# Stick-breaking attention of a two-layer trunk: triangle sums issued ahead of the next pair's scores

## What is computed

```python
z = jnp.einsum("bthd,bshd->bhts", qb, kb) * scale            # scores
log_1m = jnp.where(causal, jax.nn.log_sigmoid(-z), 0.0)
log_survive = lax.cumsum(log_1m, axis=3, reverse=True) - log_1m
w = jnp.where(causal, jnp.exp(jax.nn.log_sigmoid(z) + log_survive), 0.0)
outs.append(jnp.einsum("bhts,bshd->bthd", w, vb))
```

## Time and profile before

| | |
|---|---|
| time, median of 3 runs | 803.9 us (803.72 to 804.56) |
| time of the profiled execution | 803.06 us |
| its span | 801.3 us |
| TensorE busy | 792.3 us (99%) |
| VectorE / ScalarE / GpSimd busy | 615.6 / 438.2 / 69.9 us |
| HBM | 176 GB/s over the span |
| granted TensorE clock | 1.00 (2.4 GHz) |

### The profile page before, as it was taken

One profiled execution on the slowest core, in us unless ns is written; L12 is line 12 of the kernel. 1 busy time (PEld: TensorE's weight loads), 2 busy tenths in 40 slices (PEclk: granted clock), 3 DMA queues, 4 the chain that ended last, 5 costly groups with the idle time before them and its releaser, 6 DMA issues.

```text
span 801.3 us, 9769 instructions
## 1 busy us (share of the span) xinstructions
PE 792.3 (99%) x3770; PEld 662.9 (83%) x3770; DVE 615.6 (77%) x925; ACT 438.2 (55%) x520; POOL 69.9 (9%) x94
## 2 busy tenths in 40 slices
PE   9999999999999999999999999999999999999998
PEld 7987788888888888888888888888888888888886
DVE  6688889998757688888747878588666778888862
ACT  5667775466536544544426576757653744445430
POOL 4001013540000000000000000113420000000000
PEclk9999999999999999999999999999999999999999
DMA  7854466443456566555555544443435565565551
GB/s 246 286 165 156 136 216 212 152 159 125 158 158 195 187 196 204 182 193 210 182 185 182 186 158 157 158 137 127 153 130 166 182 206 179 192 210 184 187 208 52
DMA packets 85293, 141.38 MB, mean 176 GB/s; under 512 B 3406, under 2 KB 50672, under 8 KB 85248
## 3 DMA queue, kind: packets, MB, share of 16 engines
q1 hardware_dynamic: 84256, 139.60, 53.2%
q10 hardware_dynamic: 608, 1.06, 0.4%
q0 software_dynamic: 384, 0.11, 0.1%
HBM read 139.68 MB, written 1.07 MB: 176 GB/s over the span
## 4 chain that ended last, share of the span: by engine, by line
PE 77%; DVE 12%; ACT 5%; issue 3%; DMA 2%; SPq 0%; DVEq 0%; ACTq 0%
PE acc L1317 24%; PE acc L1319 24%; PE acc L1318 24%; DVE lo L978 4%; PE bank L1314 2%; DVE zs L1089 2%; DMA raw<-in_ssd_w_in 2%; ACT hi L661 1%; ACT zs L661 1%; DVE seg L1109 1%; ACT sq L661 1%; DVE seg L1117 1%; PE bank L1505 1%; PE bank L1483 1%; DVE hg L1109 1%
## 5 line engine op out<-in xcount | busy, mean ns | idle before, releaser
L978 DVE TENSOR_TENSOR lo<-raw,hi 128x2048 fp32r<-128x2048 f32 (+2 forms) x132 | 295.2, 2242 | 77.7 <-ACT hi L661 76.7
L661 ACT ACTIVATE hi<-raw 128x2048 fp32r<-128x2048 f32 (+2 forms) x132 | 244.8, 1861 | 93.4 <-DMA raw<-in_ffn_w_gate_up 44.1
L1317 PE MATMUL acc<-lo,aT_hi 128*128 128x512 f32 (+1 forms) x672 | 262.2, 390 | 0.5 <-DVE lo L978 0.4
L1319 PE MATMUL acc<-hi,aT_lo 128*128 128x512 f32 (+1 forms) x672 | 258.6, 385 | 0.0
L1318 PE MATMUL acc<-hi,aT_hi 128*128 128x512 f32 (+1 forms) x672 | 258.3, 384 | 0.0
L1319 PEld LDWEIGHTS acc<-hi,aT_lo 128*128 128x128 f32 x672 | 126.1, 188 | 25.5
L1317 PEld LDWEIGHTS acc<-lo,aT_hi 128*128 128x128 f32 x672 | 126.2, 188 | 25.3 <-DVE lo L978 0.6
L1318 PEld LDWEIGHTS acc<-hi,aT_hi 128*128 128x128 f32 x672 | 126.3, 188 | 24.3
L1196 DVE STREAM_TRANSPOSE uT<-un 32x256 f32<-32x256 f32 (+1 forms) x192 | 79.4, 414 | 3.1
L1317 PE MATMUL acc<-lo,uT_hi 128*128 128x512 f32 x176 | 68.6, 390 | 0.0
L1319 PE MATMUL acc<-hi,uT_lo 128*128 128x512 f32 x176 | 68.5, 389 | 0.0
(11 more groups left out here) (205 smaller groups left out, 851.7 us busy)
## 6 DMA issues: line engine op xcount, KB each, us to landing
raw<-in_ffn_w_gate_up SPq DMA_DIRECT2D x88, 512.0 KB, 4.7
raw<-in_ffn_w_down SPq DMA_DIRECT2D x22, 1024.0 KB, 4.9
raw<-in_sb_w_in SPq DMA_DIRECT2D x20, 1024.0 KB, 5.1
raw<-in_ssd_w_in SPq DMA_DIRECT2D x14, 1024.0 KB, 5.2
raw<-in_mem_w_kv SPq DMA_DIRECT2D x8, 1024.0 KB, 5.0
raw<-in_ssd_w_out SPq DMA_DIRECT2D x8, 1024.0 KB, 4.9
raw<-in_sb_w_out SPq DMA_DIRECT2D x8, 1024.0 KB, 4.9
seg<-cs_rows SPq DMA_DIRECT2D x6, 384.0 KB, 5.1
```

Source lines behind the costliest of these rows:

```text
L661: return nc.scalar.activation(out_, in_, func, **k)
L978: v.tensor_tensor(lo[w % RING][:, c], raw[w % RING][:, c], hi[w % RING][:, c].bitcast(F), ALU.subtract).then_inc(lo_ready, 1)
L1317: mm(ps, stat_hi, mov_lo, start=first, stop=False)
L1319: return mm(ps, stat_lo, mov_hi, start=False, stop=last)
```

## The change

In the units that hold both the scores of a new pair and the triangle sums of the pair before (83, 85, 87, 89, 91) the steps `sps`, `C`, `C` stand ahead of `z`, `z` in the plan. Nothing else in the code changes; the bank numbers follow from the plan.

```diff
@@ -179,12 +179,13 @@
     u = block_end("v0") + 1
     pairs = SB_HEADS // 2
     for i in range(pairs + 1):
+        if i > 0:
+            b = 2 * i - 1
+            at(u + 2 * i, ("sps", b), ("C", b - 1), ("C", b))
         if i < pairs:
             at(u + 2 * i, ("z", 2 * i), ("z", 2 * i + 1))
             at(u + 2 * i + 1, ("zd", 2 * i), ("zd", 2 * i + 1))
         if i > 0:
-            b = 2 * i - 1
-            at(u + 2 * i, ("sps", b), ("C", b - 1), ("C", b))
             at(u + 2 * i + 1, ("O", b - 1), ("O", b))
```

## The result

The changed kernel takes 805.66 us (median of 7 runs, 805.42 to 806.84) against 803.72 us (median of 7, 803.03 to 804.56): ratio 1.0027, 95% interval 1.0017 to 1.0037, that is 0.27% or 2.2 us slower, the distance between the means; the medians are 1.94 us apart. The profiled executions stand at 805.51 us (span 803.7) and 803.06 us (span 801.3), 2.4 us apart. The forecast was 806.6 us, with 0.85 for slower.

What follows compares the result with a forecast made beforehand. TensorE, busy 99% of the span, was taken to bound the kernel. Delays of 1.59 and 1.12 us sum to 2.7, on 803.9 giving 806.6 us (+0.34%); own range 805.9 to 807.3, 8 in 10 from 804.7 to 808.3.

Steps and rivals of the forecast that it cites:

- The bound: Whole span: TensorE is busy 99%; its delays between 508 and 607 us are added to the end in full.
- C is ready earlier: Units 83 to 94: C, issued 1.2 us earlier, still finds sp_lo written; slack 1.66 us in unit 83, 1.1 for C2.
- ScalarE: Unit 83: z's calls fall behind C's exps, so |z| of heads 2 and 3 starts at 528.23, 4.5 us later.
- Banks: Units 84 and 88: the hT transposes now wait for z's banks; in unit 84 these free at 531.81 and 532.86 us.
- The sum: Delays of TensorE in units 84 and 88: 1.59 + 1.12 = 2.7 us, bounds 2.0 to 3.4.
- first term: Unit 84: second hT q1 transposes start at 532.96 instead of 531.37 us, delaying everything behind by 1.59 us.
- second term: Unit 88: second hT q2 transposes start at 565.65 instead of 564.53 us, another 1.12 us.
- The waits named as signs: Transposes wait for VectorE's spb: 0.9 and 0.7 us in unit 84, about 0.4 and 0.7 in unit 88.
- Only the first place stalls: Rival: ScalarE and VectorE catch up by unit 87, so unit 88 loses nothing; +1.0 to +1.6 us, 805.4; chance 0.12.
- No slower: Rival: VectorE's subtraction of C starts earlier in units 83 and 87, O0's wait goes; 803.3 us, -0.6; chance 0.06.
- C waits for softplus: Rival: sp_lo comes late, C2 and C6 wait 0.3 to 0.9 us each; +4 to +6 us, 808.5; chance 0.13.
- the clock falls: Rival: a TensorE wait lowers its granted clock and slows the products behind it; +3 us or more; chance 0.02.

Runs made afterwards that it cites:

- TensorE's order alone: Against the kernel before: only TensorE issues C ahead of z, bank deal and ScalarE's sequence as before; 803.46 us against 803.11, ratio 1.0004.
- TensorE's order back: Against the changed kernel: TensorE issues z ahead of C again, banks and ScalarE as changed; 805.75 us, ratio 1.0028 to the kernel before.
- unit 83 alone: The kernel before with the new order of steps only in unit 83; 804.57 us against 803.11, ratio 1.0019.
- banks as before: Against the changed kernel: banks dealt out in the old order, TensorE and ScalarE as changed; 809.2 us, ratio 1.0066 to the kernel before.
- ScalarE's order back: Against the changed kernel: ScalarE does z's six calls ahead of C's exps again, TensorE and banks as changed; 803.09 us, ratio 0.9995 to the kernel before.

## Why the prediction was right

- **The bound.** Every wait of TensorE is paid in full at the end: the last stretch lies between 232.30 and 232.42 us in all ten kernels, which is no difference for spans given to 0.1 us. Shown.
- **C is ready earlier, TensorE's order is free.** No wait for `sp_lo` in any run; TensorE's order alone leaves the distances as they were. C2 was due 1.26 us behind the end of `sp_lo` (538.72 against 536.50 + 0.96), where 1.1 was worked out.
- **ScalarE.** |z| at 528.08, worked out 528.23; with the 0.16 us by which this execution is early it agrees to 0.01. Shown by its own edit.
- **Banks.** The transposes wait for L1219 at both places, and with the old deal the O products do. Shown.
- **O0** keeps its wait, 0.56 us.
- **The sum.** 1.59 + 1.12 = 2.71 us were worked out, 1.53 + 1.03 = 2.56 measured. In the first term, the part that was mis-sized is the handover from the release of a bank to TensorE's start: I took the 0.10 us seen from GpSimd to TensorE, and from VectorE it is 531.69 - 531.64 = 0.05. In the second term the handover cancels, since it also sets when TensorE arrives; there 0.06 of the 0.09 us is the subtraction, 559.14 + 0.16 = 559.30 instead of 559.36. The remaining 0.01 and 0.03 us are too small to be traced.
- **The waits named as signs.** Two pairs of L1315 for `spb` came, at both places, but smaller than named: 0.68 and 0.40 us instead of 0.9 and 0.7, then 0.18 and 0.40 instead of 0.4 and 0.7. The named sizes were delays of a start, and the profile counts as a wait only the time in which TensorE stands idle. The sum was made with the delays, so it holds.
- **From the profile to the median.** 806.6 us was forecast and 805.66 came. Of the 0.94 us, 0.15 is the sum and 0.18 the base (803.9 was the median of three runs, 803.72 that of seven). The other 0.6 us is the difference between the medians' distance, 1.94, and the traces', 2.56. By the medians the loss is just outside the forecast's own band of +2.0 to +3.4 us, and 805.66 just below its 805.9; by the distances it is well inside. Seven executions spread over 1.4 us, so that chance can do this is likely, but argued. Where more were run, the two measures agree better: 2.53 by medians and 2.62 by distances with TensorE's order back (9 and 25 executions), 1.46 and 1.53 with unit 83 alone (11 and 33). The run with banks as before doesn't fit that, 5.98 against 4.80.
- **Rivals.** "Only the first place stalls" is ruled out by the 1.03 us in unit 88, and the run with unit 83 alone shows what it would have given, 1.0019. "No slower" rested on an earlier subtraction; the changed plan gives none, but the edit that brings it, 2.2 us earlier, gives that outcome (the 1.6 us that I named as the point where it decides were not tried). "C waits for softplus" and "the clock falls" did not show: no run has a wait for `sp_lo`, and the granted clock is 1.00 in all profiled executions. The chances of the recorded list add up to 0.88 for slower (0.67, half of 0.12, 0.13 and 0.02) where 0.85 was stated; nothing hangs on it.

## What to carry to other kernels

Where one plan orders all engines, a step moved for one of them moves on all, and changes who inherits which buffer. Before moving a step, follow it on each engine's queue: here TensorE's part was worth nothing, ScalarE's caused the loss, and the deal of the banks set its size. Where an engine will stand idle for a late operand, put the independent work that is ready ahead of that wait and not behind it. Where the wait comes from a long instruction that nobody needs yet (the split of a unit that TensorE reaches later), try moving the short urgent instruction ahead of it: here that was the only edit that came out below the kernel before, by 0.48 us of distance with the change and 0.37 without it.

## What the runs showed of the hardware that was not expected

**The first inputs land up to 1.3 us later in one trace than in another.** The median of the four loads of `in_x`, from issue to landing, is 5.7 to 7.0 us in the ten traces, and the start of unit 83 follows it to about 0.1 us:

| landing of `in_x`, us | unit 83 starts at, us |
|---|---|
| 5.7 | 520.96 (ScalarE's order back) |
| 5.8 | 521.02, 521.04 (the change), 521.07 |
| 5.9 | 521.26 |
| 6.1 | 521.20 (before) |
| 6.3 | 521.56, 521.63 |
| 6.7 | 521.99 (TensorE's order alone) |
| 7.0 | 522.49 (banks as before) |

TensorE's own wait for `in_x` near 7 us is the poorer measure: it is 1.3 us where unit 83 starts at 521.99 and 0.8 us where it starts at 522.49, since waits of 0.5 us each for the first `lo` and `aT_lo` follow there. The delay is complete by the scan's first wait, whose end is at 74.48 us before and at 75.74 with banks as before. It is as large as the effects studied here, so that distances within a trace tell kernels apart that spans don't. Each kernel has a single trace, so that it belongs to the execution and not to the kernel is not shown; that executions of the kernel before spread over 1.8 us (802.66 to 804.46) speaks for it.

**The delay between GpSimd and VectorE goes both ways.** The mask of 2.82 us above starts 0.07 us behind VectorE's split and ends 0.60 us behind it. In the run with ScalarE's order back, GpSimd's masks run from 529.23 to 530.67, the split starts between them at 529.92, and it is the split that is longer, 2.89 us instead of 2.29:

```profile
529.92 2.89 DVE L984 TENSOR_TENSOR lo<-raw,hi 128x2048 fp32r<-128x2048 f32 x1 [0.36 <-ACT hi L667]
```

The kernel before has both directions, at nearly the same offset. GpSimd's two masks of `spb`, then VectorE's splits beside them:

```profile
529.48 1.42 POOL L627 TENSOR_TENSOR spb<-spb,tlt 128x256 f32<-128x256 f32 x2
...
544.67 3.55 POOL L627 TENSOR_TENSOR spb<-spb,tlt 128x256 f32<-128x256 f32 x2
```
```profile
530.15 2.89 DVE L978 TENSOR_TENSOR lo<-raw,hi 128x2048 fp32r<-128x2048 f32 x1 [0.36 <-ACT hi L661]
...
545.34 2.29 DVE L978 TENSOR_TENSOR lo<-raw,hi 128x2048 fp32r<-128x2048 f32 x1 [0.85 <-ACT hi L661]
```

The split starts 0.67 us behind the first mask both times. Once it is the split that is longer, by 0.6 us, and once the pair of masks, by 2.1 us. A schedule can't count on either.

The Trainium skill, page SBUF — State Buffer, section "SBUF: two separate sides", says that whichever of the two starts first holds the port pair for its whole instruction and the other blocks. The masks of 2.82 us agree with that, and the longer split is what it would give the other way round. Which one gets the ports when the split starts just as one mask ends and the next begins, these traces don't tell from the start times.
